# Even mixer: nineteen input products in one block, with the sliding-window attention laid between half groups of twelve of them

## What is computed

```python
def even_mixer(h, w_in, w_a2, b_a, onorm, sink, w_out, table, gla_state, cache_k, cache_v):
    q, k, v, g, lr, sq, sk, sv = jnp.split(h @ w_in, AB_SPLIT, axis=-1)   # 256 256 512 512 16 512 128 128
    loga = jax.nn.log_sigmoid((lr @ w_a2 + b_a).astype(f32)) / GLA_TAU
    ...
    S, o_a = gla_scan(q, k, v, loga)                    # gated linear attention, in chunks
    kb, vb = band_blocks(sk), band_blocks(sv)           # own chunk of 64 frames and the 2 before it
    o_b = sink_attend(qb, kb, vb, bias, sink)           # 8 query heads, 2 key heads, softmax with a sink
    o_a = rmsnorm(o_a, onorm).reshape(B, T, GLA_V) * jax.nn.silu(g.astype(f32))
    out = jnp.concatenate([o_a, o_b], axis=-1) @ w_out
```

## Time and profile before

| | |
|---|---|
| time, median of 3 runs (lowest, highest) | 4107.73 us (4105.18 to 4112.48) |
| the profiled execution, its own time | 4104.21 us |
| its span | 4102.3 us |
| mean granted TensorE clock, share of full speed | 0.932 |
| PE busy, share of the span | 87% |
| DVE, ACT, POOL busy | 38%, 27%, 15% |

### The profile page before, as it was taken

One profiled execution on the slowest core, in us unless ns is written; L12 is line 12 of the kernel. 1 busy time (PEld: TensorE's weight loads), 2 busy tenths in 40 slices (PEclk: granted clock), 3 DMA queues, 4 the chain that ended last, 5 costly groups with the idle time before them and its releaser, 6 DMA issues. The chain is left out here.

```text
span 4102.3 us, 62461 instructions
## 1 busy us (share of the span) xinstructions
PE 3551.3 (87%) x26609; PEld 3333.2 (81%) x26609; DVE 1543.5 (38%) x2368; ACT 1123.8 (27%) x2085; POOL 611.9 (15%) x877
## 2 busy tenths in 40 slices
PE   9887546798799999999889987476897799999998
PEld 8886433597699999999569877464896799999998
DVE  6211425433333223223524649545424333233233
ACT  6100233321232112112534542243312222121123
POOL 2000210010021001012121238430100111010011
PEclk9998778999899999999789999788899899999999
DMA  6321111122111111111554665874222211111111
GB/s 226 101 78 54 59 43 25 35 63 88 53 43 46 47 47 47 47 47 37 169 187 153 227 202 148 199 169 110 52 70 66 63 47 47 47 47 47 47 43 62
DMA packets 486248, 347.33 MB, mean 85 GB/s; under 512 B 117358, under 2 KB 459342, under 8 KB 482734
## 3 DMA queue, kind: packets, MB, share of 16 engines
q1 hardware_dynamic: 455658, 314.48, 27.0%
q0 software_dynamic: 10368, 19.51, 1.5%
q10 hardware_dynamic: 19956, 9.49, 0.9%
HBM read 244.65 MB, written 98.85 MB: 84 GB/s over the span
## 5 line engine op out<-in xcount | busy, mean ns | idle before, releaser
L79 PE MATMUL ps<-ff_h,ff_wh 128*128 128x352 f32 x4224 | 1009.3, 322 | 0.0
L79 PEld LDWEIGHTS ps<-ff_h,ff_wh 128*128 128x128 f32 x4224 | 730.3, 188 | 1.3
L79 PE MATMUL ps<-y_parts,ff_wh 128*128 128x352 f32 x2880 | 695.3, 323 | 16.3 <-DVE ff_wl L1504 16.3
L79 PE MATMUL ps<-ff_h,ff_wl 128*128 128x352 f32 x2112 | 676.5, 320 | 0.0
L79 PEld LDWEIGHTS ps<-y_parts,ff_wh 128*128 128x128 f32 x2880 | 504.8, 189 | 16.6 <-DVE ff_wl L1504 16.6
L79 PE MATMUL ps<-y_parts,ff_wl 128*128 128x352 f32 x1440 | 466.2, 324 | 0.0
L79 PEld LDWEIGHTS ps<-ff_h,ff_wl 128*128 128x128 f32 x2112 | 396.0, 187 | 0.0
L79 PE MATMUL ps<-rw_parts,rw_wh 128*128 128x352 f32 (+1 forms) x1152 | 290.0, 334 | 23.5 <-PEq L2937 13.0
L1888 POOL TENSOR_TENSOR ff_silu<-ff_silu,rs 128x352 f32<-128x352 f32 x132 | 126.9, 963 | 1229.4 <-ACT ff_silu L1827 1229.4
L1648 DVE TENSOR_TENSOR x<-ps,x 128x352 f32<-128x352 f32 x240 | 126.0, 525 | 485.1 <-PE ps L79 482.3
L79 PEld LDWEIGHTS ps<-y_parts,ff_wl 128*128 128x128 f32 x1440 | 272.1, 189 | 0.0
(11 more groups left out here) (388 smaller groups left out, 5667.3 us busy)
## 6 DMA issues: line engine op xcount, KB each, us to landing
ff_w<-in_ffn_w SPq DMA_DIRECT2D x120, 512.0 KB, 3.8
mixed_t<-oq_st SPq DMA_DIRECT2D x48, 176.0 KB, 1.9
rw_ra_d<-tb_rk SPq DMA_DIRECT2D x8, 1056.0 KB, 8.0
rw_kbt_d<-tb_gk SPq DMA_DIRECT2D x8, 1056.0 KB, 4.0
rw_gg_d<-tb_gk SPq DMA_DIRECT2D x8, 1056.0 KB, 6.8
fr_w<-in_xa_wk SPq DMA_DIRECT2D x8, 1024.0 KB, 5.4
fr_w<-in_xa_wv SPq DMA_DIRECT2D x8, 1024.0 KB, 5.3
oq_w<-in_xa_wq SPq DMA_DIRECT2D x16, 512.0 KB, 4.1
```

Of the source, the lines that this page charges most:

```text
L79: mm = nc.tensor.matmul(out, l, part, start=start and n == 0, stop=stop and n == 2)
```

## The change

`product`, `gate_product`, `swa_keys`, `turn_out`, `swa_bias` and `swa` go. One block, `even_products`, takes their place. It has 19 units over `Groups` with a ring of three banks: keys, values, four of queries, the low-rank one (units 0 to 6), then the twelve of GLA. Keys, values and queries stay in SBUF (`ext`, `q`). The twelve GLA units are cut into 72 halves of a group, 12 matmuls each, and the attention's steps stand between the halves: scores of chunk c after half 4c+1, the transposes of its probabilities after half 4c+6, the product with the values after half 4c+7, the copy out at 4c+8. The six gate matmuls stand after halves 3 and 4. Weights are now loaded by ACT's queue. Each chunk's scores are eight matmuls of 64 rows by 64 columns in place of four of 128 by 128; the values are turned straight from `ext`. `split_y` runs two blocks of four tiles. GLA's own blocks are unchanged, and now come last of the two.

```diff
+        groups = Groups(nc, ctx, "ab", ps, units, BLK, BLOCKS)
+        scores_at = lambda i: (i - 1) // 4 if i % 4 == 1 and (i - 1) // 4 < N else None
+        turns_at = lambda i: (i - 6) // 4 if i % 4 == 2 and i >= 6 else None
+        meets_at = lambda i: (i - 7) // 4 if i % 4 == 3 and i >= 7 else None
+        leaves_at = lambda i: (i - 8) // 4 if i % 4 == 0 and i >= 8 else None
+        HALVES = 6 * NG
...
+            def scores(c):
...
+                for p in range(4):
+                    for r in halves:
+                        mm = nc.tensor.matmul(ps[r, 3 + p // 2, p % 2 * KEYS:(p % 2 + 1) * KEYS],
+                                              q[r, p, c * CHUNK:(c + 1) * CHUNK],
+                                              ext[r, 0, at(c):at(c) + KEYS], start=True, stop=True)
+                mm.then_inc(scored, 1)
...
+            def meets(c):
+                pe.wait_ge(p_copied, c + 1)
+                pe.wait_ge(v_copied, min(c + 2, N))
...
+                for k, r in enumerate(halves):
+                    nc.tensor.matmul(ps[r, 7, 2 * P:4 * P], vt[:, c % 2, r], both[:, k], start=True, stop=False)
+                for k, r in enumerate(halves):
+                    mm = nc.tensor.matmul(ps[r, 7, 2 * P:4 * P], vt2[0:CHUNK, c % 2, r], both2[:, k], start=False, stop=True)
...
+            for j in range(GLA0):
+                for blk in range(BLOCKS):
+                    groups.sum(pe, j, blk, h)
...
+            for i in range(HALVES):
+                j, blk, part = GLA0 + i // 6, i // 2 % BLOCKS, i % 2
+                groups.sum(pe, j, blk, h, part * KT // 2, (part + 1) * KT // 2)
+                if scores_at(i) is not None:
+                    scores(scores_at(i))
...
+                if turns_at(i) is not None:
+                    turns(turns_at(i))
+                if meets_at(i) is not None:
+                    meets(meets_at(i))
...
         @block.scalar
         def _(act):
+            nc.scalar.preload_act_table_set(LN_EXP)
+            weights.load(act, 0)
+            weights.load(act, 1)
+            weights.high(act, 0)
+            weights.high(act, 1)
...
+            for i in range(HALVES):
+                j = GLA0 + i // 6
+                if i % 6 == 0:
+                    weights.high(act, j + 1)
+                    weights.load(act, j + 2)
+                if scores_at(i) is not None:
+                    exps(scores_at(i))
...
+                if turns_at(i) is not None:
+                    turned(turns_at(i))
...
         def split_y(yh):
             with nc.cleanup_on_exit():
-                split(nc, "ysplit", y, *yh)
+                for n, y in enumerate((ya, yb)):
+                    split(nc, f"ysplit{n}", y, *(part[:, 4 * n:4 * n + 4] for part in yh), 4)
```

## The result

| | before | changed |
|---|---|---|
| time, median (lowest, highest) | 4109.10 us (4105.18 to 4112.48), 4 runs | 3972.22 us (3967.61 to 3977.88), 4 runs |
| profiled execution, its own time | 4104.21 us | 3976.34 us |
| mean granted clock | 0.932 | 0.945 |

What follows compares the result with a forecast made beforehand. PE's own stream plus waits for ACT was to bound the block: 138.0 + 224.5 + 68 + 26.6 = 457.1 us at PE's end. With the later stretch, 117.5 us saved from 4107.7 gives 3990 us, range 3950 to 4035.

Steps and rivals of the forecast that it cites:

- the likeliest case: New block: PE's own stream plus a wait for ACT in each chunk, 3990 us, own range 3970 to 4010; chance 0.54.
- the rival in which the waits do not bind: New block: PE's waits for ACT vanish and overlap is perfect, 33 us more saved, 3957 us; chance 0.15.
- PE's start: Block's beginning: PE starts at 138.0 us, behind ACT's 1.28 us table load; 1.3 us come back if that hides.
- scores of a chunk: Attention on PE: score matmuls on two array quarters in turn take 1.5 us, bounds 1.3 and 2.6.
- waits of PE: Before each chunk's value matmuls, PE waits for ACT's copies: 1.26 us ten times, 2.34 six times, 26.6 us in all.
- to GLA's first DMA: End of the block: 3.5 us from PE's end at 457.1 to GLA's first DMA at 460.6.
- GLA and the splits: After the block: GLA unchanged at 179.8 us, splitting y in two blocks 13.3 us, including 2.1 for the second block.
- The product stream and chunk work: On PE: products, gate, small things and slow start sum to 224.5 us; attention 4.0 us a chunk, 68 for 17.
- The overlap of quarters: Score matmuls alternating between two array quarters overlap, by 35% or more in an earlier trace row.
- The rival of serial tiles: Quarters and halves of the array do not overlap: 41 us less saved, 4031 us, scores alone 4009; chance 0.18.
- Edits costed at nothing: Weight rounding, DVE's low parts, banks, bias table, stores and small DMAs: covered by PE's stream, 0 us.
- The rival on the slow side: Waits pull the granted clock to 1.2 GHz in the product stream; wholly so, the kernel takes 4208 us; chance 0.05.

Runs made afterwards that it cites:

- the two edits that take them away: Two separate edits of the changed kernel: ACT's copies ahead of the next chunk's exponentials, 3961.59 us; value matmuls one half later, 3960.49 us.
- copies first: Changed kernel with ACT's copies of a chunk's turned probabilities ahead of the next chunk's exponentials: 3961.59 us, ratio 0.9635.
- values at once: Changed kernel with each chunk's value matmuls straight behind the transposes of its probabilities, no half between: 4023.79 us, ratio 0.9790.
- the loop without products: Changed kernel with all 72 halves first and the 17 attention chunks after them, nothing between their steps: 4063.47 us, ratio 0.9893.
- scores by quarter: Changed kernel with all four score matmuls of one array quarter before the four of the other: 3987.12 us, ratio 0.9706.
- one border: Changed kernel with unit 4's weights asked for only once unit 3 is done: 3982.76 us, ratio 0.9697.
- one split: Changed kernel with the eight tiles of y split in one block again: 3966.14 us, ratio 0.9651.

## Why the prediction was right, and where it was off

The likeliest case was the one that came: PE's own stream plus a wait for ACT's copies in each chunk. The median lies 18 us under the forecast, inside the likeliest case's own range (3970 to 4010). The time alone doesn't settle it: the rival in which the waits do not bind stood at 3957, 15 us on the other side. It is the 16 waits on L2942, and the two edits that take them away, that speak for the likeliest case. But eleven of the waits are so short (0.37 us) that they nearly did not bind. By its steps:

| step | forecast | measured |
|---|---|---|
| PE's start | 138.0 | 136.63 |
| scores of a chunk | 1.5 | 1.44 |
| transposes of values, of probabilities | 0.25, 0.86 | 0.20, 0.79 |
| values up to the next product matmul | 1.0 and a change of shape | 1.16 (308.42 to 309.58) |
| waits of PE | 26.6 (10 x 1.26, 6 x 2.34) | 10.7 (11 x 0.37 or 0.38, 5 x 1.32) |
| PE's end | 457.1 | 444.30 |
| to GLA's first DMA | 3.5 | 2.86 |
| GLA and the splits | 193.1 | 191.59 |
| saved | 117.5 | 132.5 |

- **The waits were mis-sized, by 15.9 us.** The error at the mark is 15.0 us, and the other terms (3.5 us better, 4.5 worse) nearly cancel, which is luck. The interval on ACT's side is 302.88 to 308.42, 5.54 us, where I had 6.19. Bias addition starts 0.12 us after the scores' end, not 0.33 (I had counted the old scores at 1.28 us by their columns, where the row lasts 1.57); exponentials 2.44 after it, not 2.55; they last 1.87, not 1.95; copies take 1.11, not 1.36. The last is a fault in reading: I measured it up to 689.20 in the earlier trace rows, where the bracket says that PE then waited for DVE's `sw_vt`, not for the copies. On PE's side the interval is 302.88 to 308.05, 5.17 us, where I had 4.93, since product matmuls after a change of shape and the change before the values lie in it. 6.19 - 4.93 = 1.26 became 5.54 - 5.17 = 0.37. Four small errors, each under 0.3 us, took two thirds of the wait, because the wait is a difference of two long intervals. And c = 15 has no weights to round (they would be for a unit after the last), so five rounds are long, not six.
- **The product stream and chunk work were 4.5 us too cheap.** A round without wait is 11.74 us (copies first); less four halves of 1.91 that is 4.10 for the chunk, 4.0 forecast: 1.7 us in all. The first scores come at 224.76, 0.9 us later than my sum when it is begun at PE's true start; the gate matmuls took twice 2.04 us in place of 3.5. Another 1.1 are the 0.07 us that each of the 16 rounds with a wait takes beyond its wait, counted with the stream here.
- **The overlap of quarters was right**, and shown: 1.44 us in turn, 2.15 one quarter after the other. The rival of serial tiles (0.18) falls for scores; values, at 1.16 us for eight records with the change of shape, are far from its 2.3.
- **The start, the end and GLA** were 1.4, 0.6 and 1.5 us better. The table load hides, but a start between 135.9 and 137.7 in kernels with the same head says that part of the 1.4 is chance; of the 1.5, 0.9 are GLA's own, which also is chance, and 0.6 the splits (12.7 for 13.3). The end is 2.86 us where 3.5 was an estimate. 1.4 + 15.9 - 4.5 + 0.6 + 1.5 = 14.9 of the 15.0 us. The other 3 of the 18 us of the medians lie outside the stretch.
- **Edits costed at nothing** cost PE no wait: in copies first it is busy for every microsecond of 213, so weights loaded by ACT, DVE's low parts, bank emptying, the bias table and small DMAs all stay hidden. HBM reads fell from 244.65 to 241.40 MB and writes from 98.85 to 95.61; no row of waits answers to them.
- **The rival on the slow side** (0.05) did not come in this kernel, but my argument against it was weak. I had said that the old loop, idle 1.40 us in 6.82, kept 0.95. Waits of 2.3 to 3.3 us in each round of the new stream cost another 24.3 us by the clock (values at once), and in the loop without products 4.2 us of idle time took the clock to 0.67. The changed kernel's five waits of 1.32 us stay clear of it; with scores by quarter three of the same five did not. Even so no kernel here came out slower than before: the rival's price of 117.5 us was never reached.

## What to carry to other kernels

When filler work is laid between the steps of a serial chain, compute the wait that is left as the difference of two intervals and give it the sum of all their errors as its range; read each interval from rows whose bracket names the releaser that you mean. On the engine that serves the chain, put what the busiest engine waits for ahead of what it will want later: here two lines of order on ACT were worth 9.8 us with filler, and 61 us without. A wait on PE can cost more than its length through the granted clock, so read the clock in stretches of a few microseconds behind each wait, not only as a mean.

## What the hardware showed that was not expected

- The granted clock inside a product stream can fall to its lower level behind a single wait of 1.32 us: three times of five with scores by quarter, never of fifteen with scores in turn (the changed kernel, one border, one split). With waits of 2.29 us some rounds fell and others did not. What decides it is open.
- Score records one quarter after the other take 0.134 us for 192 columns, less than the 0.161 us that the full-array rate gives. Whether some records still overlap there was not tried.
- At changes of tile shape the record of weight loads has short stops with no wait on another engine: 0.22 us ahead of scores and of the last chunk's values, 0.28 ahead of the transposes of values, 0.38 or 0.39 between the two kinds of value matmuls and behind them. Ahead of the transposes of probabilities, which use the full array like the products, there is none.
